# Expert weights as contraction halves on one queue, and a column-tiled down product, in a two-layer trunk with expert-choice experts

## What is computed

```python
def expert_choice_ffn(x, w_router, w_gate, w_up, w_down):
    cap = CAP_FACTOR * T // N_EXPERTS            # 16 of 128, 64 of 512
    aff = softmax(x @ w_router)
    gsel, idx = lax.top_k(swapaxes(aff, 1, 2), cap)
    xs = x[bidx, idx]
    hdn = silu(einsum('becd,edf->becf', xs, w_gate)) * einsum('becd,edf->becf', xs, w_up)
    out = einsum('becf,efd->becd', hdn, w_down) * gsel[..., None]
    return zeros_like(x).at[bidx, idx].add(out)

for i in range(2):                               # the trunk
    sh1, sc1, g1, sh2, sc2, g2 = modulation(cond, w_ada[i], b_ada[i])
    x = x + g1 * mixer(rmsnorm(x, norm1_g[i]) * (1 + sc1) + sh1)
    h = rmsnorm(x, norm2_g[i]) * (1 + sc2) + sh2
    x = x + g2 * expert_choice_ffn(h, w_router[i], w_gate[i], w_up[i], w_down[i])
```

## Time and profile before

| | |
|---|---|
| time, median of 3 runs | 3105.9 us (3104.97 to 3121.13) |
| time of the profiled execution | 3121.28 us |
| span of the profiled execution | 3119.4 us |
| mean granted TensorE clock | 0.945 |
| TensorE matmuls (PE) | 2752.9 us, 88% |
| TensorE weight loads (PEld) | 1914.8 us, 61% |
| VectorE, ScalarE, GpSimd | 963.2, 576.8, 95.8 us |
| moved by DMA | 547.61 MB, mean 176 GB/s |

### The profile page before, as it was taken

The page is one execution under the profiler, slowest core; times in us unless marked ns, Lnnn a source line. Parts: engine busy times, 40 slices in busy tenths (PEclk is TensorE's granted clock), DMA queues, the critical chain, the costliest instruction groups (busy, mean ns, idle before and its releaser), DMA issues.

```text
span 3119.4 us, 59648 instructions
## 1 busy us (share of the span) xinstructions
PE 2752.9 (88%) x26597; PEld 1914.8 (61%) x26597; DVE 963.2 (31%) x2408; ACT 576.8 (18%) x1297; POOL 95.8 (3%) x145
## 2 busy tenths in 40 slices
PE   6999999986988888896999999999989688888884
PEld 1465469944666656661456549999975466666663
DVE  1100126645111111102177626766754311111113
ACT  3100111142000000003167212222234000000002
POOL 0000000000000000000000000000000000000000
PEclk9999998887999999998999999999989799999997
DMA  8411100036999999968411100000022899999993
GB/s 285 169 55 54 48 0 1 1 74 228 331 352 336 334 328 328 324 229 275 170 55 55 39 2 1 1 1 1 1 68 75 300 344 339 341 342 341 337 346 111
DMA packets 276494, 547.61 MB, mean 176 GB/s; under 512 B 15233, under 2 KB 23817, under 8 KB 276233
## 3 DMA queue, kind: packets, MB, share of 16 engines
q1 hardware_dynamic: 175049, 328.64, 30.6%
q10 hardware_dynamic: 93600, 188.75, 16.5%
q0 software_dynamic: 7584, 26.22, 3.4%
HBM read 517.89 MB, written 25.70 MB: 174 GB/s over the span
## 4 chain that ended last, share of the span: by engine, by line
PE 83%; DVE 6%; issue 6%; ACT 3%; DMA 2%; SPq 0%; DVEq 0%; POOL 0%; ACTq 0%
PE ps L1206 20%; PE ps L1217 14%; PE ps L803 9%; PE ps L813 7%; PE ps L760 5%; PE ps L1139 4%; PE ps L1101 3%; PE ps L804 2%; PE ps L1083 2%; PE ps L880 2%; PE ps L1115 1%; PE ps L966 1%; PE ps L962 1%; PE ps L950 1%; PE ps L791 1%
## 5 line engine op out<-in xcount | busy, mean ns | idle before, releaser
L1206 PE MATMUL ps<-wk,slots 128*64 128x80 f32 x12288 | 451.1, 234 | 84.6 <-issue 84.6
L1206 PEld LDWEIGHTS ps<-wk,slots 128*64 128x64 f32 x12288 | 436.5, 138 | 119.5 <-issue 118.0
L1217 PE MATMUL ps<-qkv,og 128*80 128x512 f32 x1024 | 453.6, 601 | 2.2 <-DVE og L1750 1.3
L803 PE MATMUL ps<-hT,slots 128*128 128x512 f32 x640 | 334.0, 604 | 3.1 <-ACT hT L455 3.1
L1217 PEld LDWEIGHTS ps<-qkv,og 128*80 128x80 f32 x1024 | 153.2, 152 | 276.8 <-issue 274.2
L1206 PE MATMUL ps<-wk,qkv 128*64 128x80 f32 x4096 | 173.1, 247 | 67.2 <-issue 67.2
L804 PEld LDWEIGHTS ps<-hT,slots 128*128 128x128 f32 x640 | 123.2, 193 | 156.7 <-issue 156.7
L813 PE MATMUL ps<-slots,hT 128*128 128x512 f32 x480 | 209.7, 597 | 0.0
L1206 PEld LDWEIGHTS ps<-wk,qkv 128*64 128x64 f32 x4096 | 165.2, 148 | 71.7 <-issue 71.7
L760 PE MATMUL ps<-slots,cnd 128*2 128x512 f32 x384 | 172.4, 604 | 35.7 <-DVE x L1778 24.6
L1726 DVE COPY idc<-idT 80x1 uint32 (+1 forms) x32 | 4.8, 150 | 632.0 <-DMA moe_d<-og,idc 632.0
(11 more groups left out here) (261 smaller groups left out, 3171.5 us busy)
## 6 DMA issues: line engine op xcount, KB each, us to landing
slots<-in_w_gate_dram ACTq DMA_DIRECT2D x60, 2048.0 KB, 12.3
qkv<-in_w_down_dram SPq DMA_DIRECT2D x34, 2048.0 KB, 20.5
slots<-in_w_up_dram SPq DMA_DIRECT2D x32, 2048.0 KB, 14.6
qkv<-in_w_up_dram SPq DMA_DIRECT2D x32, 2048.0 KB, 9.6
qkv<-in_w_down_dram ACTq DMA_DIRECT2D x30, 2048.0 KB, 8.7
slots<-in_w_ada_dram SPq DMA_DIRECT2D x24, 2048.0 KB, 8.0
slots<-in_w_in_dram SPq DMA_DIRECT2D x16, 2048.0 KB, 8.5
slots<-in_w_out_dram SPq DMA_DIRECT2D x4, 2048.0 KB, 16.2
```

Of the source, the lines that this page charges most:

```text
L803: mm(PS[:, b, :], w, hT[:, kt, P:TOK], start=(kt == 0), stop=(kt == KT - 1))
L1206: ins = mm(PS[64 * s:64 * s + 64, j, fb * CAP:(fb + 1) * CAP], slot[j][:, kt, c:c + 64], xsT[q][:, kt, :], start=(kt == 0), stop=(kt == KT ...
L1217: ins = mm(PS[0:CAP, 4 + j, :], hdT[:, ft, :], slot[4 + j][:, ft, :], start=(ft == 0), stop=(ft == KT - 1))
```

## The change

- `w_expert` gives halves of the contraction with all 1024 columns (`wide[j]` is 4 x 1024 for each partition), in the order gate 0, gate 1, up 0, up 1, down 0, down 1. For gate and up, partition p holds rows 8p to 8p + 7, so a half is one run of 16 KB for each partition. For down, the rows stay as they were, in runs of 4 KB.
- All six loads are issued by SyncE in order of use, j = 0 to 3 each when `hidden` of the expert before has used that buffer, j = 4 and 5 both at the end of its `down`. ScalarE issues none.
- `hidden` runs the same 256 matmuls in another order, each sum over two buffers; gate lies in PSUM banks 0 and 1, up in 2 and 3. A new semaphore `up_low` lets VectorE start on the lower half.
- `down` becomes two products: the 64 sample tokens as two 64-column tiles side by side, each with 512 columns moving (16 matmuls), then the 16 prompt tokens as four 32-column tiles, each with 256 columns moving (32 matmuls). ScalarE copies out two 64 x 512 and four 16 x 256 pieces, and `pick` makes seven small copies in place of two.
- Rows 8p + k as the order of the contraction reach back: `turn`, `turn_tile` for k = 1 and the modulation's units 6 to 9 take every 8th column as the stationary operand; those four units do it with 8 plain matmuls in place of 4 transposes. The router weights are loaded likewise, and three small loads and one VectorE addition for each layer join the setup and the modulation.

```diff
         def w_expert(L, e, j):
-            name, hf = (("w_gate", 0), ("w_up", 0), ("w_gate", 1), ("w_up", 1), ("w_down", 0), ("w_down", 1))[j]
-            return a[name][L].rearrange("e (k p) n -> e p k n", p=P)[e, :, :, hf * HC:(hf + 1) * HC]
+            name, kh = (("w_gate", 0), ("w_gate", 1), ("w_up", 0), ("w_up", 1), ("w_down", 0), ("w_down", 1))[j]
+            w = a[name][L].rearrange("e (k p) n -> e p k n" if name == "w_down" else "e (p k) n -> e p k n", p=P)
+            return w[e, :, 4 * kh:4 * kh + 4, :]
...
+                    (n2g[:, :, :], a["norm2_g"].rearrange("l (p k) -> p l k", p=P)),
+                    (b2g[:, :, 0:KT], a["b_ada"][:, 3 * D:4 * D].rearrange("l (p k) -> p l k", p=P)),
+                    (b2g[:, :, KT:2 * KT], a["b_ada"][:, 4 * D:5 * D].rearrange("l (p k) -> p l k", p=P)),
...
-                    for j in range(6) if first else (1, 3, 5):
+                    for j in range(6):
                         if not first:
-                            sp.wait_ge(S("moe_used"), L * PER["moe_used"] + e * 6 + (j - 5))
-                        sp.dma_start(slot[j], w_expert(L, e, j)).then_inc(land[j], 16)
+                            sp.wait_ge(S("moe_used"), L * PER["moe_used"] + e * 6 + (min(j, 4) - 5 + (j >= 4)))
+                        sp.dma_start(wide[j], w_expert(L, e, j)).then_inc(land[j], 16)
...
                     for hf in range(2):
-                        A(osb[q][0:CAP, hf * HC:(hf + 1) * HC], PS[0:CAP, 4 + hf, :], ACT.Copy,
-                          scale=gsc[q][0:CAP, :]).then_inc(S("o_ready"), 1)
-                        if hf == 0:
-                            load(4)
+                        A(osb[q][0:CAPS, hf * HC:(hf + 1) * HC], PS[64 * hf:64 * hf + 64, 4, :], ACT.Copy,
+                          scale=gsc[q][64 * hf:64 * hf + 64, :]).then_inc(S("o_ready"), 1)
+                    act.wait_ge(S("moe_used"), L * PER["moe_used"] + e * 6 + 6)
+                    for c in range(4):
+                        A(osb[q][CAPS:CAP, c * 256:(c + 1) * 256], PS[32 * c:32 * c + CAPP, 5, 0:256], ACT.Copy,
+                          scale=gsp[q][32 * c:32 * c + CAPP, :]).then_inc(S("o_ready"), 1)
...
+                    if 6 <= n < 10:
+                        by_k = mrow[n % 2].rearrange("c (p k) -> c k p", k=KT)
+                        for k in range(KT):
+                            blk = 24 + (n - 6) // 2 * KT + k
+                            ins = mm(PS[64 * (n % 2):64 * (n % 2) + 64, 6, 2 * blk:2 * blk + 2], by_k[:, k, :], ident[0:2, 0:2],
+                                     start=True, stop=True)
...
+                        col = o[:, t, :].rearrange("q (p k) -> q k p", k=KT)[:, b, :] if k else o[:, t, b * P:(b + 1) * P]
+                        ins = tr(PS[:, 2 * (t % 2) + 2 + j, kt * P:(kt + 1) * P], col, ident)
...
-                        ins = tr(PS[:, 6 + kt // 4, (kt % 4) * CAP:(kt % 4 + 1) * CAP], xs[q][0:CAP, kt * P:(kt + 1) * P], ident[0:CAP, 0:CAP])
+                        ins = tr(PS[:, 6 + kt // 4, (kt % 4) * CAP:(kt % 4 + 1) * CAP], xs[q][0:CAP, :].rearrange("c (p k) -> c k p", k=KT)[:, kt, :], ident[0:CAP, 0:CAP])
...
+                        for i in range(4 * KT):
+
+                            kt, fb = (i // KT, i % KT) if j % 2 == 0 else (i % 4, i // 4)
+                            for s in range(2):
+                                c = fb * P + 64 * s
+                                ins = mm(PS[64 * s:64 * s + 64, j // 2 * 2 + fb // 4, (fb % 4) * CAP:(fb % 4 + 1) * CAP],
+                                         wide[j][:, kt, c:c + 64], xsT[q][:, 4 * (j % 2) + kt, :],
+                                         start=(j % 2 == 0 and kt == 0 and fb % 4 == 0), stop=(j % 2 == 1 and kt == 3),
+                                         skip_group_check=True)
...
+                    for ft in range(KT):
+                        for j in range(2):
+                            ins = mm(PS[64 * j:64 * j + 64, 4, :], hdT[:, ft, 0:CAPS], wide[4 + ft // 4][:, ft % 4, j * HC:(j + 1) * HC],
                                      start=(ft == 0), stop=(ft == KT - 1))
+                    ins.then_inc(S("o_mm"), 1)
+                    if not first:
+                        pe.wait_ge(S("o_ready"), L * PER["o_ready"] + e * 6)
+                    for ft in range(KT):
+                        for c in range(4):
+                            ins = mm(PS[32 * c:32 * c + CAPP, 5, 0:256], hdT[:, ft, CAPS:CAP],
+                                     wide[4 + ft // 4][:, ft % 4, c * 256:(c + 1) * 256],
+                                     start=(ft == 0), stop=(ft == KT - 1))
+                    ins.then_inc(S("moe_used"), 2)
...
-                    V.tensor_copy(gsc[q][0:CAP, :], gsel[0:CAP, bass.ds(e, 1)]).then_inc(S("idx"), 1)
+                    for hf in range(2):
+                        V.tensor_copy(gsc[q][64 * hf:64 * hf + 64, :], gsel[0:CAPS, bass.ds(e, 1)])
+                    for c in range(4):
+                        ins = V.tensor_copy(gsp[q][32 * c:32 * c + CAPP, :], gsel[CAPS:CAP, bass.ds(e, 1)])
+                    ins.then_inc(S("idx"), 1)
```

More of the change, by code:

```diff
@@ L48 @@
 PER = dict(ada_ev=12, fin_r=5, fin_i=5, ab=1, ada_mm=12, afft=1, aff=1, fin_sq=5, fin_start=1, g1b=4, g1e=4, g2b=4,
-           gathered=256, gexp=32, gmm=1, h_chain=32, hidden=32, idx=16, logits=1, moe_used=96, o_ready=32,
+           gathered=256, gexp=32, gmm=1, h_chain=32, hidden=32, idx=16, logits=1, moe_used=96, o_ready=96, o_mm=16, up_low=16,
            omm=10, scattered=256, selt=1, sel=2, sme=1, sm=1, st_new=4, topk=1, x_moe=5, x_new=10, xs_a=64,
@@ L88, in backbone @@
         slot = [s.rearrange("p (k n) -> p k n", k=KT) for s in SL]
+        wide = [s.rearrange("p (k n) -> p k n", k=KT // 2) for s in SL]
         wk = sb("wk", [P, 4608])
@@ L128, in backbone @@
         gsc = [sb(f"gsc{q}", [P, 1]) for q in range(2)]
+        gsp = [sb(f"gsp{q}", [P, 1]) for q in range(2)]
         xn_d = nc.dram_tensor("xn_d", [TOK, D], F32, kind="Internal").ap()
@@ L675, in experts, with expert @@
                 A(aff[:, :, :], aff[:, :, :], ACT.Exp).then_inc(S("sme"), 1)
[L677 to L681, removed]
+                def expert(e, q, first):
+                    act.wait_ge(S("moe_used"), L * PER["moe_used"] + e * 6 + 2)
+                    if first != 0:
+                        act.wait_ge(S("hidden"), L * PER["hidden"] + e * 2)
                     for hf in range(2):
[L684 to L688, removed]
-                    for hf in range(2):
-                        act.wait_ge(S("moe_used"), L * PER["moe_used"] + e * 6 + (5 + hf))
-                        if hf == 0 and first is None:
-                            act.wait_ge(S("scattered"), L * PER["scattered"] + (e - 1) * 16)
-                        A(osb[q][0:CAP, hf * HC:(hf + 1) * HC], PS[0:CAP, 4 + hf, :], ACT.Copy,
-                          scale=gsc[q][0:CAP, :]).then_inc(S("o_ready"), 1)
-                        if hf == 0:
-                            load(4)
+                        A(eb[hf], PS[:, hf, 0:320], ACT.Tanh, scale=0.5).then_inc(S("gexp"), 1)
+                    act.wait_ge(S("o_mm"), L * PER["o_mm"] + e + 1)
+                    if first is None:
+                        act.wait_ge(S("scattered"), L * PER["scattered"] + (e - 1) * 16)
+                    for hf in range(2):
+                        A(osb[q][0:CAPS, hf * HC:(hf + 1) * HC], PS[64 * hf:64 * hf + 64, 4, :], ACT.Copy,
[4 more added lines that the diff above has]
+                          scale=gsp[q][32 * c:32 * c + CAPP, :]).then_inc(S("o_ready"), 1)
                 expert(0, 0, 0)
@@ L703, in experts @@
                 expert(EX - 2, 0, None)
-                expert(EX - 1, 1, None, last=True)
+                expert(EX - 1, 1, None)
             def modulation(L):
@@ L1199, in hidden @@
                         pe.wait_ge(land[j], e * 16 + (16 * moe_base(L, j) + 16))
[L1200 to L1207, removed]
+                        for i in range(4 * KT):
[6 more added lines that the diff above has]
+                                         skip_group_check=True)
+                            if j == 3 and kt == 3 and fb == 3:
+                                ins.then_inc(S("up_low"), 1)
                         ins.then_inc(S("moe_used"), 1)
```

42 lines of the change are left out of this document (24 added, 18 removed).

## The result

The changed kernel takes 3131.8 us (median of 13 runs, 3118.9 to 3138.3), the kernel before in the same comparison 3115.7 us (13 runs, 3105.0 to 3121.1). The ratio is 1.005, with a 95% interval of 1.0034 to 1.0066: slower by 16 us, where 3015 us, 100 us faster, were forecast. The time lies 7 us outside the range.

What follows compares the result with a forecast made beforehand. Transfers were taken as the bound behind PE, 35.3 of 39.06 us an expert. Terms −3.4 − 0.5 + 0.7 gave 35.9 us; over 32 experts −101, +10 outside: 3030 profiled, 3015 us median, 8-in-10 range 2945 to 3125.

Steps and rivals of the forecast that it cites:

- Down product: In `down` of each expert: the two new products take 10.5 us instead of 13.9, −3.4 us.
- two-group rival: Prompt product: four column groups overlap only by two, it takes 6.9 us, no change at 3120 us; chance 0.10.
- 128 more PE instructions, half a packet: In `down`: added instructions hide in the main product at best, cost half a 1.6 us stall at worst; +0.4 us taken.
- +0.2 for each expert: Expert stages: −0.5 us from longer runs and +0.7 from more instructions and fuller transfers, apart from the product's gain.
- signs of being wrong: Profile after: stalls of 3.5 us or more, prompt product of 7 us, `turn` of several us, DMA releaser ahead of `hidden`.
- 5 us remain: cost 0: From `down` through scatter and gather to `turn`: added evictions and copies fit in the slack, costing nothing.
- 7.5 us to spare: Between the gather's landing, 8.0 us after its issue at 1017.85, and `turn` at 1033.40: the slack read before the change.
- From 0 to several times; I take 0: Transposes in `turn` and `turn_tile` k = 1: 336 now load every 8th column; extra cost taken as 0.
- +8: Modulation, eight units over both layers: 4 transpose records become 16, 0.33 to 1.3 us each, +8 us.
- forecast +10 for all outside the experts: Modulation and setup together, with three small loads and two VectorE additions: +10 us, range 2 to 30.
- Longer runs: Weight loads in expert stages: 408 GB/s instead of 387 shortens waits ahead of instruction packets, −0.5 us an expert (0 to −0.8).
- runs rival: Instruction packets in `hidden` wait by runs, not bytes: stalls grow 2.35 us each, some 3300 us; chance 0.12.

Runs made afterwards that it cites:

- the runs with 2 KB: The changed kernel with each load issued as two column halves, 3097.1 us; the same with packed transposes and the old contraction order for gate and up, 3067.5 us.

## Why the prediction was wrong, point by point

*Down product: right.* Forecast 10.5 us, measured 7.0 to 7.1 + 3.6 = 10.7; four column groups do run at once. From 13.9, over 32 experts, 104 us. With the loop written out on both sides, the product alone gives 69 us on two queues (3078.9 to 3009.5), where PE then waits 38 us for loads; with 4 KB runs on one queue it is 112 us (to 2967.0), in which the loads' part is not separated. The two-group rival falls.

*"128 more PE instructions, half a packet ... at worst half a packet costs half a stall ... I take +0.4": wrong, the first step that failed.* I counted packets evenly and did not look at the loop. A jump back takes 3.3 to 3.8 us of fetching here, as it did before (3.5 to 4.9). The prompt product leaves only its last 1.4 us to cover it, so that 2.2 to 2.8 us stand open at each of ten jumps, and in the second stage 4.6 to 5.5 more, nine records behind it. Written out, the changed kernel gains 67 us and the kernel before 36: 31 us of the gain went there. What the 36 us of the kernel before are is shown in part only: 28 us less idle ahead of `hidden`, with 18 instruction packets fewer. Idle ahead of `hidden` as a whole rose by 5 us, where the forecast's +0.2 for each expert made 6: the number came out by luck, as the stalls inside `hidden` became fewer (two in place of three in most experts without the jump), and no run tells why. Of the signs of being wrong that the prediction named, stalls of 3.5 us or more came, and a DMA releaser, ahead of `turn` and not of `hidden`.

*"5 us remain: cost 0" for the tokens' chain: wrong, the second, and in the profile the larger.* I sized evictions and copies, but took the gather's 8.0 us as fixed and the stretch from `down` to `turn` as 0.5 us shorter. And the 7.5 us to spare were read in the expert with the longest stretch of the 28 between two of them, 27 us; the median is 24.5, which leaves 5. Measured in the stretch above: evictions to scatter 2.9 us in place of 1.6, scatter 9.4 against 8.7, copies to gather's issue 2.1 against 1.1, gather 11.1 against 8.0; 25.5 us in place of 19.4, beside a `hidden` of some 21 us in the experts that wait. An expert that begins behind a stalled jump takes 27 to 32 us to its `turn`, and there the gather is in time; so the two costs take turns. Moving `turn`, with the loop written out, gives 43 us back. Packets of 16 KB make it late: with 2 KB runs from the same queue it lands after 7.7. The Trainium skill ("DMA: Bandwidth & Descriptors", Queues, rings and completion order) has each engine serve its queues in turn by packets. The gather agrees, 10.6 us behind long runs and 7.7 behind short ones; the instruction packets, with 1.15 to 1.30 MB ahead in place of 1.06, do not show it.

*"From 0 to several times; I take 0" for strided loads: wrong.* A weight load went from 140 to 206 ns, `turn` from 0.70 to 1.05 us, 11 us over 32 experts. The modulation's four units turn in 2.0 us instead of 0.33:

```profile
86.95 2.01 PE ps L755 x16
```

1.7 us eight times, 13 us, where +8 were forecast. In the profiled pair the first layer's half does not show (the first `turn` of the experts comes at 774.3 us after, 774.5 before), and 9 us more lie between the two expert stages, so the forecast +10 for all outside the experts was near. All of it together is the 30 us between the runs with 2 KB. In their profiles the first `turn` comes 11 us later with the order 8p + k, 9 us more lie between the stages, and `turn` takes 11 us more; the first of these three moves by several us from one kernel to the next. The Trainium skill ("SBUF — State Buffer", Door 1) speaks of a penalty at this stride; the 66 ns are its size here.

*Longer runs: −0.5 us each and the rival.* 4 KB in place of 2 KB gave 14 us over all, close to 32 x 0.5. 16 KB in place of 2 KB cost 35 us, with the late gather. The runs rival had the right cause and the wrong victim: not the instructions, but the gather. (The forecast's 1104 matmuls of an expert count each record together with its weight load; they are 552 records.)

*The sum.* −104 for the product, +31 for the edge, +43 for the late gather with the clock behind it, +30 for the strided order: about 0, where 16 us more were measured. These four come from different surroundings, the 43 without the loop and the 30 with 2 KB runs, and need not add up. In the two profiled executions the sum closes: −82 for the products (−103 at full clock, +21 for the lower clock), +53 of idle ahead of `turn`, +11 for `turn` itself, +5 of idle ahead of `hidden`, −1 for its records and +9 between the stages are −5, and the spans differ by −2.3. So most of the gain went to the idle time ahead of `turn` and the lower clock, 74 us. The medians lie 18 us further apart than these two executions do, and no trace holds those. The forecast of a gain of 100 us came from taking two unknown costs, the tokens' chain and the strided loads, at nothing, and from not seeing the third, the jump.

## What to carry to other kernels

When a slow stretch is made fast, ask what it was covering. Here 13.9 us of few, slow instructions covered the 3.5 to 4.9 us of the loop's jump back, and `hidden` with its stalls left the tokens' chain some 5 us to spare; the change used up both at once. Read such a margin from many turns of the loop and not from one. Runs of 4 KB gave what long runs had to give; runs of 16 KB delayed the gather that the next step waits for, and the order of rows that they need made every later transpose strided. If a loop's body ends in many short instructions, try it written out before judging the change.

## What was not expected of the hardware

- A jump back in TensorE's loop took 3.3 to 6.7 us by its branch record in every kernel here that has the loop, and 0.08 us where the loop ended. The instruction packet was served 0.9 to 4.2 us after the branch began, 0.9 to 1.0 where no data moved and 3.4 behind 1.11 MB, and the branch ended 2.4 to 2.8 us later. What shows of it depends on what is still running: nothing behind the old product, 2.2 to 5.4 us behind the prompt product, and up to 10.5 us (4.7 + 5.8) when the next packet boundary lies nine records further on. Written out, 65 to 87 us went away in kernels with the fast product, 36 in the kernel before.
- Four 16-row tiles in column groups ran fully side by side: 64 records of 256 columns in 3.6 us.
- A gather of 80 rows of 4 KB landed after 10.6 to 11.0 us beside 16 KB runs and after 7.6 to 8.1 beside runs of 2 or 4 KB on the one queue.
- After 4.3 us without work PE ran its next 5 us at 1.2 GHz (granted 0.50 to 0.53), a further 1.6 us for such a wait.
- Weight loads of every eighth float32 took 206 ns, packed ones 140.
